# Hybrid encoder step: first and second halves of the forgetting values made a step after their rows, second halves of output weights moved behind the next step's minima

## The reference

```
u = rmsnorm(h);  z = u @ w_in                       # q, k, v of both groups, forget gates
A: forgetting attention, 8 heads x 64, causal:  softmax(q k^T * s + c_i - c_j) v,  c = cumsum(log f)
   (the 32 new rows see 256 cached rows as well)
B: sliding-window attention, 8 query heads, 2 kv heads, relative bias, sinks
h = h + concat(rmsnorm(A), rmsnorm(B)) @ w_out
h = h + (silu(n @ w_gate) * (n @ w_up)) @ w_down,   n = rmsnorm(h)
y = rmsnorm(h)
```

## Time and profile before

| what | us |
|---|---|
| median of 3 runs | 1428.67 (1427.84 to 1430.19) |
| the profiled execution | 1427.94, of which its span is 1426.1 |
| PE busy | 1387.8 (97%) |
| DVE, ACT, POOL busy | 576.9 (40%), 481.4 (34%), 213.4 (15%) |
| stretch 214:462, steps -9 to 44 and a half | PE busy 242.2 of 248.0 |
| stretch 462:482, steps 45 to 47 | PE busy 14.0 of 20.0, granted clock 0.74 |

### The profile page before, as it was taken

One profiled execution on the slowest core, in us unless ns is written; L12 is line 12 of the kernel. 1 busy time (PEld: TensorE's weight loads), 2 busy tenths in 40 slices (PEclk: granted clock), 3 DMA queues, 4 the chain that ended last, 5 costly groups with the idle time before them and its releaser, 6 DMA issues.

```text
span 1426.1 us, 22599 instructions
## 1 busy us (share of the span) xinstructions
PE 1387.8 (97%) x9041; PEld 1287.2 (90%) x9041; DVE 576.9 (40%) x1378; ACT 481.4 (34%) x1049; POOL 213.4 (15%) x317
## 2 busy tenths in 40 slices
PE   6999999999999899999999999999999999999997
PEld 5989898788888677889999999999999999999997
DVE  6345634242323433662343424242525252525156
ACT  6346555655554652553212121212121111121103
POOL 3145551634443330000000000000000000000000
PEclk9999999999999899999999999999999999999999
DMA  7621124212120444314202020202020202020003
GB/s 199 116 69 38 32 73 158 84 43 80 52 82 16 149 163 150 106 45 123 74 16 75 15 74 16 74 15 75 16 74 16 74 20 72 26 76 16 16 1 122
DMA packets 110256, 97.64 MB, mean 68 GB/s; under 512 B 15937, under 2 KB 96929, under 8 KB 109641
## 3 DMA queue, kind: packets, MB, share of 16 engines
q1 hardware_dynamic: 110152, 96.20, 23.2%
HBM read 77.07 MB, written 19.21 MB: 68 GB/s over the span
## 4 chain that ended last, share of the span: by engine, by line
PE 90%; DVE 3%; DMA 3%; ACT 2%; issue 2%; POOL 1%; SPq 0%; ACTq 0%; DVEq 0%
PE ps L602 28%; PE ps L603 26%; PE ps L604 26%; PE ps L806 2%; PE ps L736 1%; PE ps L953 1%; DMA cb<-c_scratch 1%; DMA ob<-o_scratch 1%; PE ps L818 1%; PE ps L683 1%; DVE ps L1645 1%; PE ps L897 1%; PE ps L774 1%; ACT sp_x L1276 0%; PE ps L701 0%
## 5 line engine op out<-in xcount | busy, mean ns | idle before, releaser
L1892 DVE TENSOR_TENSOR outs<-outs,ps 128x384 f32<-128x384 f32 (+1 forms) x264 | 134.4, 509 | 108.1 <-PE ps L604 107.8
L1878 DVE TENSOR_TENSOR gu<-ps,sg 128x384 f32<-128x384 f32 (+1 forms) x66 | 34.6, 524 | 237.6 <-PE ps L604 237.6
L2062 POOL TENSOR_TENSOR pl_x<-sp_x,ph_x 128x512 fp32r<-128x512 f32 (+5 forms) x120 | 102.2, 865 | 168.0 <-ACT sp_x L1276 166.7
L1456 ACT ACTIVATE h_hi<-gu 128x384 fp32r<-128x384 f32 (+1 forms) x66 | 32.9, 498 | 222.2 <-DVE gu L1878 222.2
L1275 ACT ACTIVATE ph_x<-ps,negc 128x512 fp32r<-128x512 f32 (+5 forms) x120 | 62.9, 524 | 83.6 <-PE ps L818 83.6
L1450 ACT ACTIVATE sg<-ps 128x384 f32<-128x384 f32 (+1 forms) x66 | 30.4, 465 | 171.7 <-PE ps L604 171.7
L602 PE MATMUL ps<-f_hi,ff0hi 128*128 128x384 f32 (+1 forms) x264 | 85.7, 325 | 0.0
L602 PE MATMUL ps<-f_hi,ff1hi 128*128 128x384 f32 (+1 forms) x264 | 85.6, 324 | 0.0
L602 PE MATMUL ps<-f_hi,ff2hi 128*128 128x384 f32 (+1 forms) x264 | 85.6, 324 | 0.0
L602 PE MATMUL ps<-f_hi,ff3hi 128*128 128x384 f32 (+1 forms) x264 | 85.6, 324 | 0.0
L603 PE MATMUL ps<-f_lo,ff0hi 128*128 128x384 f32 (+1 forms) x264 | 85.3, 323 | 0.0
(11 more groups left out here) (311 smaller groups left out, 3770.8 us busy)
## 6 DMA issues: line engine op xcount, KB each, us to landing
raw<-in_w_gate SPq DMA_DIRECT2D x22, 512.0 KB, 4.7
raw<-in_w_up SPq DMA_DIRECT2D x22, 512.0 KB, 4.8
raw<-in_w_down SPq DMA_DIRECT2D x22, 512.0 KB, 3.9
raw<-in_w_in SPq DMA_DIRECT2D x14, 512.0 KB, 4.1
cb<-c_scratch SPq DMA_DIRECT2D x4, 1312.0 KB, 7.2
xt<-in_x_prompt SPq DMA_DIRECT2D x8, 512.0 KB, 4.2
out<-outb SPq DMA_DIRECT2D x16, 256.0 KB, 2.9
ob<-o_scratch SPq DMA_DIRECT2D x16, 256.0 KB, 3.1
```

The source lines that it names most:

```text
L1456: act.activation(h_hi[par][:, f, c0:c0 + n], gu[(f + c) % 2][:, 0:n], ACT.Copy).then_inc(S["g_hi"], 1)
L1878: dve.tensor_tensor(gu[(f + c) % 2][:, 0:n], bank(3 + c, n), sg[c][:, 0:n], ALU.mult)\
L1892: add = dve.tensor_tensor(y, y, bank(b, whole * P).rearrange("p (t m) -> p t m", t=whole), ALU.add)
L2062: pool.tensor_tensor(pl_x[at][0:rows, 0:n], sp_x[at][0:rows, 0:n], ph_x[at][0:rows, 0:n].bitcast(F32), ALU.subtract).then_inc(S["x_pl"], 1)
```

## The change

1. The ninth tile of values is turned in the same part as tiles 4 to 7 (part 3 of step 15i; step -6 for pair 0).
2. First halves of values leave the task on ACT and are made in the next step, behind its exponentials, from `outb`; they raise a counter of their own, `v_hi`.
3. Second halves of values wait for `v_hi`, raise `v_lo`, and stand in DVE's next step behind its minima and behind the output weights' halves, before parts 2 to 4; all steps now have that order.
4. Second halves of output weights are made in the step after their first halves, behind its minima.
5. Stores of values wait for the copy (`fv_out`); the products with values, the reuse of `outb` and the reload of the value cache wait for `v_lo`.

```diff
-VALUES_AT = [(0, 2 - LEAD, 3, (0, 4)), (0, 3 - LEAD, 3, (4, 4)), (0, 4 - LEAD, 0, (8, 1))]
+VALUES_AT = [(0, 2 - LEAD, 3, (0, 4)), (0, 3 - LEAD, 3, (4, 4)), (0, 3 - LEAD, 3, (8, 1))]
 for _i in range(1, PAIRS):
-    VALUES_AT += [(_i, NFU * _i - 2, 3, (0, 4)), (_i, NFU * _i, 3, (4, 4)), (_i, NFU * _i + 1, 0, (8, 1))]
+    VALUES_AT += [(_i, NFU * _i - 2, 3, (0, 4)), (_i, NFU * _i, 3, (4, 4)), (_i, NFU * _i, 3, (8, 1))]
-BY_ACT = ("sk", "ck", "sv", "bias", "amw", "amx", "fk", "fc", "fv", "tb")
-BY_DVE = ("ck", "sv", "negc", "otw", "otx", "fc", "fv", "tb")
+BY_ACT = ("sk", "ck", "sv", "bias", "amw", "amx", "fk", "fc", "tb")
+BY_DVE = ("ck", "sv", "negc", "otw", "otx", "fc", "tb")
...
# PE, fox_values
-                        pe.wait_ge(S["ev_act"], act_done(T_OF["fv", i, *a]))
-                        pe.wait_ge(S["ev_dve"], dve_done(T_OF["fv", i, *a]))
+                        pe.wait_ge(S["v_lo"], rows_out(T_OF["fv", i, *a]))
...
# ACT, store_free (reuse of outb)
-                        act.wait_ge(S["ev_dve"], dve_done(STORES[o - 2]))
+                        act.wait_ge(S["v_lo"], rows_out(STORES[o - 2]))
...
# ACT: taken out of the task, into a function of its own
                     out.then_inc(S["fv_out"], 1)
-                    act.wait_ge(S["fv_out"], rows_out(n))
-                    (waits and first halves, as below)
+            def values_hi(*place):
+                for item, a in plan(*place):
+                    if item == "task" and TASKS[a[0]][0] == "fv":
+                        ...
+                        if t0 == 8:
+                            act.wait_ge(S["cv_in"], 16 * (i + 1))
+                            act.activation(vw_hi[:, 9:11, 0:3:2, :], cache_v[:].rearrange(...), ACT.Copy)
+                        act.wait_ge(S["fv_out"], rows_out(n))
+                        rows = outb[STORES.index(n) % 2][0:m, 0:count, :]
+                        act.activation(vw_hi[0:m, t0:t0 + count, 0:3:2, :], rows.rearrange(...),
+                                       ACT.Copy).then_inc(S["v_hi"], 1)
...
                 if 0 <= v < NX:
                     fox_exp(v)
+                values_hi("x", v - 1, 3)
+                values_hi("x", v, 0)
                 for part in (1, 2, 3):
...
# DVE, the loop over steps (out_weights_lo: the loop over OUT_AT that stood at its end)
+                if v >= 0:
+                    items("x", v, 0, but="fv")
+                items("x", v, 1)
+                out_weights_lo(v - 1)
+                values_lo(v - 1, 3)
+                values_lo(v, 0)
+                for part in (2, 3, 4):
+                    items("x", v, part, but="fv")
                 if v == ROOT_AT:
                     roots_b()
...
# SP, store_rows and after_tasks
-                sp_.wait_ge(S["ev_act"], act_done(n))
+                if kind == "fv":
+                    sp_.wait_ge(S["fv_out"], rows_out(n))
+                else:
+                    sp_.wait_ge(S["ev_act"], act_done(n))
...
                     if kind == "fv" and a[1] == 8 and a[0] + 1 < PAIRS:
-                        sp_.wait_ge(S["ev_dve"], dve_done(n))
+                        sp_.wait_ge(S["v_lo"], rows_out(n))
                         load_fox_cache(a[0] + 1, False)
```

More of the change, by code:

```diff
@@ L541, in build @@
         names = """xin0 xin1 xin2 gain_in gw_in g_final_in a_sq a_ms a_rt a_ri a_xn a_t a_hi a_lo const_p const_d misc_in
-            win_in ck_in cv_in raw_in0 raw_in1 raw_in2 wf_in cw_hi cw_lo g_pe ev_act ev_dve fv_out pr_pe pr_act pr_dve
+            win_in ck_in cv_in raw_in0 raw_in1 raw_in2 wf_in cw_hi cw_lo g_pe ev_act ev_dve fv_out v_hi v_lo pr_pe pr_act pr_dve
             f_mm f_ev f_t f_chain f_act f_bt f_c c_out c_in band_ps band_sb band_out band_in bias_ready
@@ L834, in fox_values @@
                     pe.wait_ge(S["ev_dve"], dve_done(LAST_LEAD))
+                    pe.wait_ge(S["fv_out"], rows_out(LAST_LEAD))
                 elif first:
@@ L1160, in task @@
                 b = 4 + BANK_OF["task", n]
-                if kind not in BY_ACT:
+                if kind not in BY_ACT and kind != "fv":
                     return
@@ L1212, in task @@
                     out.then_inc(S["fv_out"], 1)
-                    act.wait_ge(S["fv_out"], rows_out(n))
[L1214 to L1223, removed]
+            def values_hi(*place):
+                for item, a in plan(*place):
+                    if item == "task" and TASKS[a[0]][0] == "fv":
+                        n = a[0]
+                        i, t0, count = TASKS[n][1]
+                        m = rows_of(t0)
+                        if i >= 1:
+                            act.wait_ge(S["x_pv"], 2 * (NFU * (i - 1) + {0: 8, 4: 12, 8: NFU}[t0]))
+                        elif t0 == 0:
+                            act.wait_ge(S["w_pv"], 2 * NWU)
+                            act.wait_ge(S["w_ttr"], 4 * NWU)
+                        if t0 == 8:
+                            act.wait_ge(S["cv_in"], 16 * (i + 1))
+                            act.activation(vw_hi[:, 9:11, 0:3:2, :], cache_v[:].rearrange("p n (h d) -> p n h d", h=2), ACT.Copy)
+                        act.wait_ge(S["fv_out"], rows_out(n))
+                        rows = outb[STORES.index(n) % 2][0:m, 0:count, :]
+                        act.activation(vw_hi[0:m, t0:t0 + count, 0:3:2, :], rows.rearrange("p n (h d) -> p n h d", h=2),
+                                       ACT.Copy).then_inc(S["v_hi"], 1)
             def items(*place):
@@ L1572, in task @@
                     hi, lo = (vs_hi, vs_lo) if kind == "sv" else (vw_hi, vw_lo)
-                    dve.wait_ge(S["ev_act"], act_done(n))
                     rows = ps[0:m, b, 0:count * P].rearrange("p (n d) -> p n d", n=count)
-                    if kind == "fv":
+                    if kind == "sv":
+                        dve.wait_ge(S["ev_act"], act_done(n))
+                    else:
+                        dve.wait_ge(S["v_hi"], rows_out(n))
                         rows = outb[STORES.index(n) % 2][0:m, 0:count, :]
@@ L1581, in task @@
                                       rows.rearrange("p n (h d) -> p n h d", h=2),
-                                      hi[0:m, t0:t0 + count, 0:3:2, :].bitcast(F32), ALU.subtract).then_inc(S["ev_dve"], 1)
+                                      hi[0:m, t0:t0 + count, 0:3:2, :].bitcast(F32), ALU.subtract).then_inc(S["ev_dve" if kind == "sv" else "v_lo"], 1)
                 elif kind == "tb":
@@ L1706, in values_lo, with out_weights_lo @@
                         task(*a)
+            def out_weights_lo(v):
+                for k in range(KB):
+                    if OUT_AT[k] == v:
+                        dve.wait_ge(S["cw_hi"], SPLIT_OUT + k + 1)
+                        dve.scalar_tensor_tensor(out=wo_lo[:, k, :], in0=raw2d[k % 3], scalar=gw_col[:, OUT_K[k]:OUT_K[k] + 1],
+                                                 in1=wo_hi[:, k, :].bitcast(F32), op0=ALU.mult, op1=ALU.subtract)\
+                           .then_inc(S["cw_lo"], 1)
             def items(*place, but=None):
```

## The result

The changed kernel takes 1441.21 us (median, 1439.96 to 1442.35), the kernel before, beside it on the same chip, 1428.79: a ratio of 1.0085 with a 95% interval of 1.0072 to 1.0099, so 12.4 us slower. The prediction said slower, at 1437.6, with a range of 1433 to 1441: the median lies at its upper edge, 0.2 us above it. The profiled executions took 1439.96 and 1427.94, spans 1438.1 and 1426.1: 12.0 us to be found.

The account below looks back on a forecast made before the run. TensorE (PE), busy 97% of the span, was taken as the bound, so only its idle time or clock counts. Terms 2.8 + 4.1 + 2.4 - 0.4 + 0 = +8.9 us gave a median of 1437.6 us, range 1433 to 1441.

Parts of the forecast that it names:

- Lead, row loads: Lead-in: value-cache reload now ahead on SP delays loads of rows 4 and 5, PE loses +2.8 us (+2.0 to +3.2).
- Clock in the lead: Lead-in: PE's clock does not fall in the two gaps, 0 us; +2.1 if it does.
- Rival B: The clock also falls in the lead, +2.1 us, 1439.7 us in all; chance 0.25.
- Pairs 1 and 2: Steps 16 and 31: minima now come ahead of the ninth tile's halves, -0.4 us in all (0 to -0.6).
- Step 46: Hole at step 46: minima come earlier but PE waits later for the head's bank, 0 us (-0.5 to +0.3).
- Output product: Step 47: first output product waits for output halves now behind DVE's minima, +4.1 us (+3.5 to +4.5).
- Its clock: Step 47: clock falls in the output product's wait, half clock behind it costs +2.4 us (0 to 2.6).
- C: Clock stays up after the step 47 wait, 2.4 us less, 1435.2 us; chance 0.13.
- D: Lead-in row loads cost nothing because ACT's squares can take them late, 2.8 us less, 1434.8 us; chance 0.08.
- E: Step 47: output product hardly waits because DVE gets ahead, 1431.1 us; chance 0.06.
- F: Not slower: step 46's hole closes, head's bank is out in time, clock never falls; -0.6 us, 1428.1 us; chance 0.08.

Follow-up runs that it names:

- e6: Changed kernel with one added wait: POOL's subtraction in step 46 waits for DVE's second half of the ninth values' tile; 1440.51 us (ratio 1.0078).
- e11: Changed kernel with only pair 0's ninth values' tile, its store and the cache reload back in part 0 of step -5; 1435.96 us (ratio 1.0047).
- e4: Kernel before with only the second halves of output weights two and three moved behind step 47's minima; 1436.93 us (ratio 1.0059).
- e1: Changed kernel with only pair 0's value-cache reload on SP put back behind the loads of rows 4 and 5; 1435.62 us (ratio 1.0045).
- e7: Changed kernel, cache reload and output halves 2 and 3 put back; heads straight behind step 46's minima on DVE, values' first halves at ACT's step end; 1431.31 us.
- e9: As e7, but the second half of output weight 0 moved on DVE straight behind step 46's minima, ahead of the heads; 1428.49 us (ratio 0.9990).
- e8: As e7, but the output product starts in step 48 and output halves 2 and 3 stand behind step 47's minima; 1432.93 us (ratio 1.0023).
- e10: As e7, but the second half of output weight 0 moved on DVE ahead of step 46's minima; 1428.58 us (ratio 0.9995).
- e2: Changed kernel with only output halves 2 and 3 put back to the end of DVE's step 46; 1434.65 us (ratio 1.0038).

## Why the prediction was right in kind and 3.6 us short

By its own steps, each with what the offsets show:

- **Lead, row loads, 2.8.** The reload stood at 237.10; without the 0.76 us of the start that is 236.34, forecast 236.3. The rows went 2.9 late, and the product at line 774 behind them came 3.0 late. Right, in place and size. What the text left out is how the parts share it: "the rows' loads" cost 2.9 us only because halves and tile moved together.
- **Clock in the lead, 0.** This is the step that failed. "I take no fall" was wrong: the clock fell, and the offset without the start goes from 3.0 to 4.5, so +1.5. Rival B, which had +2.1 and a chance of 0.25, is what happened, at 0.6 less than its price.
- **Pairs 1 and 2, -0.4.** From +5.29 at line 806 of step 1 to +4.91 at line 806 of step 46 (466.43 and 471.34): right.
- **Step 46, 0, bounds -0.5 and +0.3.** The mechanism was right: no wait on ACT's copy, 1.50 us for the minima (1.4 said), 4.72 for the head (3.8 said). The term was mis-sized by 0.95 (from +4.91 to +5.86). Its durations came from rows in which no subtraction of POOL stood beside DVE's output halves; in the changed order POOL's subtraction stands beside them instead of beside the minima, and both last longer. In e6, in which they stand apart, the same stretch is 1.5 us shorter (-0.6 in place of +0.95). The upper bound should have held this.
- **Output product, 4.1, at most 4.5.** The offset rises by 4.22 from line 695 (+5.86 to +10.08). Between the two the full clock came back a little earlier than before, which gives back 0.2: the product at line 774 (478.67 before, 484.30 after) stands at +5.63, and from there it is 4.45. The halves took 3.00 us, not 2.48, again beside POOL. Shown by undoing it (-6.6 us) and by doing it alone (+7.4 us in the median, +6.7 by offsets), both with the clock's part.
- **Its clock, 2.4.** From +10.08 to +12.34: 2.3. Right, with some luck: in e11, e4, e1 and e6 the same stretch cost 1.9, 2.2, 2.4 and 2.8.
- **Not in the sum: 0.8 us at the start**, in code that the change leaves alone, from the later end of half clock. In the twelve traces of other kernels the input weights' load near 228 us goes between 0.2 (e7) and 1.8 us (e9) later than in before's, and in nearly the order in which their half clock ends. So it belongs to the execution, not to the change, and 12.0 less 0.8 is what the change did in these two traces. The medians differ by 12.4 all the same; no run says what share of that is the start's.

Together: 0.8 + 3.0 + 1.5 - 0.4 + 0.9 + 4.2 + 2.3 = 12.3 at step 48, and 0.3 us less by the end.

The Trainium skill, page "TensorE: Matmul & The Clock Gate", section "What's actually happening", says that the instant of a clock change is not tied to the kernel's start and varies from run to run. The traces agree in three places. At the start, half clock ends between 21.4 (before) and 24.9 us (e9) in the same code. In the stretch 462:498, e1 and e11 do the same work in the same order and have a clock of 0.76 and 0.81. And ahead of line 701 (at 301.53 us before, up to 307.83 in the others) all thirteen traces have the same wait of 1.05 us; the clock falls behind it in e4, e7, e8 and e10 (0.86 in 300:312), at 1.6 us each, and stays full in the other nine. In the lead they do not show it. There the stretch 240:252 has 0.86 in the changed kernel, e2 and e6, the three in which the rows go 2.9 us late, and 1.00 in before and all nine others. So in the lead the fall went with the longer waits (2.17 and 1.28 us in the changed kernel), and rival B deserved more than its 0.25. But three traces cannot say that it always does, where another place shows both outcomes for one wait.

Rivals C, D and E are out: the clock did fall behind the wait, the loads did cost, the product did wait. Of F, the first half came true (the wait on the copy went) and the second did not: line 695, which needs the head's bank, came 5.3 us behind line 701. e7 shows that this wait can be removed, by putting the heads ahead of the 2.5 us of output halves, and e9 what it needs besides. The clock fell in step 46 in both all the same (line 695 takes 1.11 and 1.12 us).

## What to carry to other kernels

When work is moved behind a waiting instruction on a queue that issues everything in order, price the wait by what its releaser now has ahead of it, not by the move alone: the same reload ahead of the same loads cost 1.0 us with the halves made at once and 2.9 us with them a step later. When operand halves are moved out from under one consumer, look for the next one that needs them, and for the buffer that they free: here the second halves fed an output product 3 us away, and the first of them held the buffer of weights still to come. A duration from a row holds for the neighbours that the instruction had there; after a reorder, read which engine will stand beside it. And before the offset between two traces is laid to an edit, see whether it begins in code that the edit leaves alone.

## What the runs showed of the hardware

**DVE and POOL slow each other.** Two output halves (two SBUF inputs each) took 2.48 us alone, and 3.00, 3.17, 3.21 or 3.81 beside POOL's work; one took 1.87 where 1.26 was usual; a values' half took 1.48 for 0.68. POOL's two subtractions of 128x384 took 1.96 apart from DVE's halves and 2.93 or 3.35 beside them (in e7 they kept 1.96, and only DVE's halves grew, to 3.17), and a cast of 128x8 took 1.20 instead of 0.20. The minima of 128x512, which read PSUM, took 0.68 to 0.76 us in steps 46 and 47 of all the traces, whatever POOL did. The Trainium skill, page "SBUF — State Buffer", section "Who interferes with whom", has a rule for this: the ports that DVE and GpSimd share are an exclusive lock, a DVE instruction with two SBUF inputs contends for them with a GpSimd instruction that reads SBUF, and the order of issue decides which one is blocked. The traces agree to 0.2 us, if the later one waits for the whole of the other: in e9 POOL began at 471.87 with two instructions of 0.98 us; a DVE half that arrived at 472.07 and waited until 472.85 would end at 474.11 with its 1.26, and ended at 473.94.

**The clock costs by where the wait stands, and not in every execution.** The lead's fall cost 1.5 us, the one behind the output product 2.3. The same wait of 1.05 us, at 301.53 us in before, cost 1.6 us of clock in four traces of thirteen and nothing in nine; up to step 47, e4 does the same as the kernel before. At the start the same code ended its half clock between 21.4 and 24.9 us, which put all behind it 0.2 to 1.8 us later than in before. So two traces can differ by some 2 us with no change between them.
